# The second RMS norm's factor is taken out of the turned x and put back at the gate and behind the down product

## The reference, cut to what matters

```
x = x + m @ w_out                                      # 2048 x 2048
h = x * rsqrt(mean(x*x, axis=-1) + 1e-6) * norm2_w     # the second norm: one factor r per token
x = x + (silu(h @ w_ffn_gate) * (h @ w_ffn_up)) @ w_ffn_down   # 2048 x 5632, twice, and 5632 x 2048
```

## Time and profile before

| | |
|---|---|
| time, median of 3 runs | 2487.36 us (2487.17 to 2497.38) |
| time of the profiled execution | 2485.11 us |
| its span in the profile | 2483.2 us |
| PE busy | 2417.0 us, 97% of the span |
| DVE busy, ACT busy, POOL busy | 1518.9, 1130.0, 194.4 us |
| granted TensorE clock over the span | 0.994 of full speed |

### The profile page before, as it was taken

How to read it: one execution, slowest core, us unless ns; L and a number is a source line. 1 busy time by engine, 2 the same in 40 slices (tenths; PEclk the granted TensorE clock), 3 DMA queues, 4 the chain that set the end, 5 groups by cost and what they waited for, 6 DMA issues and landing times.

```text
span 2483.2 us, 42677 instructions
## 1 busy us (share of the span) xinstructions
PE 2417.0 (97%) x18297; PEld 2147.6 (86%) x18297; DVE 1518.9 (61%) x1890; ACT 1130.0 (46%) x1562; POOL 194.4 (8%) x198
## 2 busy tenths in 40 slices
PE   7999999999999999999999999999999999999997
PEld 7777889999888888888888899889888899899886
DVE  4899955565555655556544445745745568456556
ACT  5565545554444444444443434533544535334442
POOL 4000000001000000000000001220000061301000
PEclk9999999999999999999999999999999999999998
DMA  8444454455646666666666676434537674335465
GB/s 238 136 145 144 153 153 128 128 171 184 194 148 190 183 184 197 188 193 188 193 189 192 189 224 179 120 99 118 168 103 238 176 215 140 98 109 151 126 198 170
DMA packets 259405, 412.28 MB, mean 166 GB/s; under 512 B 53072, under 2 KB 74064, under 8 KB 258704
## 3 DMA queue, kind: packets, MB, share of 16 engines
q1 hardware_dynamic: 254496, 395.57, 53.6%
q0 software_dynamic: 4400, 13.89, 2.0%
q10 hardware_dynamic: 320, 0.08, 0.0%
HBM read 403.17 MB, written 6.30 MB: 165 GB/s over the span
## 4 chain that ended last, share of the span: by engine, by line
PE 89%; DVE 6%; ACT 2%; issue 2%; DMA 0%; ACTq 0%; SPq 0%; DVEq 0%
PE banks L578 88%; DVE wp_hl L1126 2%; ACT wp_hl L1808 1%; DVE r_SA L1664 0%; PE banks L801 0%; DMA xt<-x 0%; DVE r_SA L1630 0%; DVE rsd L1275 0%; DVE nsd L1542 0%; DVE r_kb L1632 0%; ACT L1808 0%; PE banks L695 0%; DVE xr L1801 0%; DVE xr L1799 0%; DVE sqr L1285 0%
## 5 line engine op out<-in xcount | busy, mean ns | idle before, releaser
L578 PE MATMUL banks<-XX_hl,wp_hl 128*128 128x256 f32 (+1 forms) x10112 | 1424.7, 300 | 10.4 <-DVE wp_hl L1126 9.2
L1126 DVE TENSOR_TENSOR wp_hl<-raw,wp_hl 128x1024 fp32r<-128x1024 f32 x740 | 913.9, 1242 | 826.3 <-ACT wp_hl L1808 825.7
L578 PEld LDWEIGHTS banks<-XX_hl,wp_hl 128*128 128x128 f32 x10112 | 1319.7, 190 | 89.7 <-issue 15.4
L1808 ACT ACTIVATE wp_hl<-raw 128x1024 fp32r<-128x1024 f32 x740 | 781.4, 1059 | 1057.3 <-PE banks L578 1034.5
L578 PE MATMUL banks<-wp_hl,FF_hl 128*128 128x512 f32 x1056 | 240.4, 389 | 0.0
L578 PEld LDWEIGHTS banks<-wp_hl,FF_hl 128*128 128x128 f32 x1056 | 197.9, 188 | 41.0
L578 PE MATMUL banks<-wp_hl,XX_hl 128*128 128x512 f32 x576 | 139.1, 398 | 0.0
L578 PEld LDWEIGHTS banks<-wp_hl,XX_hl 128*128 128x128 f32 x576 | 107.6, 190 | 28.1 <-issue 5.3
L578 PE MATMUL banks<-wp_hl,MXa_hl 128*128 128x512 f32 x384 | 88.3, 389 | 0.0
L578 PE MATMUL banks<-wp_hl,MM_hl 128*128 128x512 f32 x384 | 87.4, 389 | 0.0
L578 PEld LDWEIGHTS banks<-wp_hl,MM_hl 128*128 128x128 f32 x384 | 71.9, 188 | 15.2 <-DVE wp_hl L1126 0.3
(11 more groups left out here) (432 smaller groups left out, 1884.3 us busy)
## 6 DMA issues: line engine op xcount, KB each, us to landing
raw<-w_in SPq DMA_DIRECT2D x304, 512.0 KB, 3.8
raw<-w_out SPq DMA_DIRECT2D x96, 512.0 KB, 4.5
raw<-w_ffn_gate SPq DMA_DIRECT2D x88, 512.0 KB, 4.3
raw<-w_ffn_up SPq DMA_DIRECT2D x88, 512.0 KB, 4.2
raw<-w_ffn_down SPq DMA_DIRECT2D x88, 512.0 KB, 4.2
raw<-w_proj_attn SPq DMA_DIRECT2D x16, 512.0 KB, 4.2
raw<-w_proj_ssm SPq DMA_DIRECT2D x16, 512.0 KB, 3.7
raw<-w_glu SPq DMA_DIRECT2D x8, 512.0 KB, 3.7
```

Of the source, the lines that this page charges most:

```text
L578: return e.matmul(o, lhsT, rhs, start=start, stop=stop, skip_group_check=True)
L1126: return tt(d, src, hi, SUB)
L1808: return e.activation(o, x, func, bias=bias, scale=scale)
```

## The change

The turned x is no longer scaled: each quarter of `wo` is turned three pieces later with the identity, in the middle of the next job, and the factor comes in at two other places. As a row over all partitions, `rrow` (ones times the diagonal, a product on PE and a copy), it is multiplied into the summed gate, before the Silu; as a scalar per partition it is multiplied into the down product where that is added to x. The up product stays unscaled, since the factor at the end makes up for it. `wo3` isn't treated apart any more, and ACT's early load of the table for the square root is gone.

```diff
-    HALF, HLF = ("wo3", "xo30", "xo31"), marks("half", "h")
+    HALF, HLF = ("xo30", "xo31"), marks("half", "h")
...
+    RRT, RRV, FGV = marks("rrow_t", "t"), marks("rrow_v", "c"), marks("f_norm", "r")
...
     # PE, turned_x
-            if stage < 2:
+            if stage == 0:
                 e.wait_ge(*XD("d", stage))
-            elif stage == 2:
-                e.wait_ge(*freed(f"fd{g // 2}", 1))
+            elif stage < 3:
+                e.wait_ge(*freed(f"{('wo', 'fd')[stage - 1]}{g // 2}", 1))
...
-                    if stage < 2:
+                    if stage == 0:
                         last = mm(B[b][:, o:o + 128], src, dg[:, 128 * t:128 * t + 128], o == 0, o == 384)
                     else:
                         last = e.transpose(B[b][:, o:o + 128], src, ident)
...
     # PE, its list
         at.limit("wo3")
-        main(at.until("wo3"))
-        at.limit("fd3")
-        entered(1)
+        for c in range(4):
+            main(at.until(f"wo{c}"))
+            if c == 3:
+                at.limit("fd3")
+            main(at.go(6))
+            turned_x(1, 2 * c)
+            turned_x(1, 2 * c + 1)
+        bank(4, *RRV("c"))
+        e.wait_ge(*XD("d", 1))
+        for t in range(2):
+            last = mm(B[4][:, 128 * t:128 * t + 128], M["ones"], dg[:, 128 * t:128 * t + 128], t == 0, t == 1)
+        last.then_inc(RRT.made("t"), 1)
...
     # DVE, evac of wo and fd
-                    tt(x, x, b[i], ADD).then_inc(s_evV, 1)
+                    if n == "wo":
+                        tt(x, x, b[i], ADD).then_inc(s_evV, 1)
+                    else:
+                        stt(out=x, in0=b[i], scalar=rs[:, 2 + i:3 + i], in1=x, op0=MUL, op1=ADD).then_inc(s_evV, 1)
...
     # DVE, evac of fg, behind its four reductions
+                for i in range(2):
+                    g = v2(gt[2 * (c % 2) + i])
+                    e.wait_ge(*RRV("c"))
+                    e.wait_ge(s_evV, j.freed[2 * i + 1][1])
+                    tt(g, g, wide3(rrow, 2, 256), MUL).then_inc(FGV.made("r", 2 * c + i), 1)
...
     # DVE, its list
-        main(at.until("wo3"))
-        at.limit("fd3")
-        split(OF["wo3"].over + 2)
-        roots(1)
-        for g in range(10):
-            if g < 8:
-                rest_of_x(1, g)
-            if g > 1:
-                main(at.go(2))
+        for c in range(4):
+            main(at.until(f"wo{c}"))
+            if c == 3:
+                at.limit("fd3")
+            main(at.go(6))
+            if c == 3:
+                roots(1)
+            rest_of_x(1, 2 * c)
+            rest_of_x(1, 2 * c + 1)
+        e.wait_ge(*RRT("t"))
+        e.tensor_copy(rrow, B[4][:, 0:256]).then_inc(RRV.made("c"), 1)
...
     # ACT, evac of fg
-                    e.wait_ge(s_evV, j.freed[2 * i + 1][1])
+                    e.wait_ge(*FGV("r", 2 * c + i))
                     act(gt[2 * (c % 2) + i], gt[2 * (c % 2) + i], ACT.Silu).then_inc(FGA.made("s", 2 * c + i), 1)
...
     # ACT, its list
-        main(at.until("wo2"))
-        e.preload_act_table(ACT.Sqrt)
-        main(at.until("wo3"))
-        at.limit("fd3")
-        roots(1)
-        for g in range(10):
-            if g < 8:
-                rounded_x(1, g)
-            if g > 1:
-                main(at.go(2))
+        for c in range(4):
+            main(at.until(f"wo{c}"))
+            if c == 3:
+                at.limit("fd3")
+            main(at.go(6))
+            if c == 3:
+                roots(1)
+            rounded_x(1, 2 * c)
+            rounded_x(1, 2 * c + 1)
```

More of the change, by code:

```diff
@@ L313, in program @@
     FF = Pair("FF", 44 * T)
-    gt = [alloc(f"gt{i}", 512) for i in range(4)]
+    gt, rrow = [alloc(f"gt{i}", 512) for i in range(4)], alloc("rrow", 256)
     at[0] = (ARENA - 1024) // 8 * 8
@@ L1264, in main @@
                 if i:
-                    if p + 3 < NP and not (t + 1 == ENDS[j.name] and j.name in ("wo3", "xo30")):
+                    if p + 3 < NP and not (t + 1 == ENDS[j.name] and j.name == "xo30"):
                         split(p + 3)
```

## The result

| | before | changed |
|---|---|---|
| median | 2492.67 us (8 runs, 2484.73 to 2497.38) | 2502.18 us (8 runs, 2500.41 to 2504.45) |
| profiled execution, span | 2485.11, 2483.2 us | 2503.97, 2502.2 us |
| granted clock over the span | 0.994 | 0.991 |

The ratio is 1.0044, with a 95% interval of 1.0032 to 1.0056: 0.44% slower, within the half percent. It goes with the means, which differ by 11.0 us; the medians differ by 9.5, or 0.38%. The eight times of before are three from ahead of the prediction and five taken beside the changed kernel; their median is 5.3 us above that of the first three.

A forecast was written before the change was run, and what follows sets the result against it. PE, busy 97% of the span, was taken to bound the kernel. Gate 9.7 and front 1.0 make 10.7 us more, from a median of 2487.4 to 2498 us (0.43% slower); range 2490 to 2504.

The forecast's parts named there:

- its likeliest case: Whole kernel: front and gate terms hold, median 2495 to 2502 us; the forecast of 2493 to 2499.8 had chance 0.48.
- The first wait of the front: Between wo3 and fg0: PE stands still until the additions free wo3's banks, starting 3.65 us behind the last matmul.
- The second wait: In fg0, behind the last two turns: PE idles 2.88 us for the diagonal, the root's table load hidden.
- The clock: At the front's two waits: first fall costs about 2.75 us again, second 0 to 2.75, taken as 1.4.
- the full 2.75 worse: At the front: by the skill's rule of paying each long wait anew, two waits instead of one cost 2.75 us more.
- A wait under 1.8 leaves the clock alone: At PE's gate waits: waits of about 0.85 us, below 1.8, do not bring the granted clock down.
- The front as a whole: From wo3 into fg0: 0.4 us gained, 1.4 lost to the clock, +1.0 us in sum, ends -3.2 and +3.6.
- Its rival, that early turning gives the wait back: At the front: PE runs from wo3 into fg0 without a stop, median 2491.7 us; chance 0.07.
- The gate: Behind gate jobs: Silus 1.19 us later, PE stands still 0.85 behind ten jobs and 1.19 behind fg2: 9.7 us.
- the 2 and the 13 that the prediction names as signs of being wrong: PE's idle time from 740 to 1215 us: near 2 us refutes the gate part, above 13 the slack of 0.34.
- The down product: On DVE at the down job's addition: scalar with two inputs takes 676 ns against 0.68 us plain, so costs nothing.
- the unit: PE's time for one piece of a wide job, read from ACT's splits as 2.77 us each.

The follow-up runs named there:

- e2: The changed kernel without the products at the gate, the Silus waiting for the reductions as before: 2491.55 us, ratio 0.9998 to before.
- e5: The changed kernel with wo3 treated apart again and the factor made behind the first piece of fg0, two pieces earlier: 2494.85 us, ratio 1.0021 to before.
- e1: The kernel before plus only the two gate products per gate job, by a row of ones, the Silus waiting for them: 2503.62 us, ratio 1.0036 to before.
- e3: The changed kernel with the two Silus of a gate job put behind ACT's next split, all products kept: 2493.05 us, ratio 0.9998 to before.
- e8: The kernel before, unchanged, run once more for a second profile: 2492.35 us in one run, gate stretch 475.0 us.
- e6: The changed kernel with the edits of e3 and e5 together: 2480.55 us, ratio 0.9968 to before.
- e7: As e6, with the small operations of the angles spread over three pieces as well: 2476.97 us, ratio 0.9962 to before.
- e9: As e7, with four of the turns put between wo3 and fg0 to cover PE's wait there: 2484.42 us, ratio 0.9972 to before.
- e10: As e9, with the ones product ahead of the last two turns instead of behind them: 2476.11 us, ratio 0.9937 to before.
- e4: The kernel before with the angles' small operations spread over three pieces and ACT's sine and cosine four pieces later: 2486.84 us, ratio 0.9974 to before.

## Why the prediction was right, and where its steps were not

The forecast was 0.43% slower with 2498 us; measured are 0.44% and 2502.18. That lies in the stated range of 2490 to 2504, but above the 2493 to 2499.8 of the forecast and 0.2 above the 2495 to 2502 of its likeliest case. By its steps:

- **The first wait of the front** was to be 3.65 behind the last matmul of `wo3` and ended by the additions. It was 3.97 and ended by them. The additions were done 3.62 behind that matmul, where the sum has 3.59, but PE went on 0.35 behind them where the sum has 0.06. The gate waits do not show this delay.
- **The second wait**, 2.88 forecast, is 2.80, and the table load lies where the sum has it, hidden. By the drain that the Trainium skill adds to a load (ScalarE: Activation LUTs, "What ACT_TABLE_LOAD costs") the root would have come 1.2 us later, an estimate; the trace has it 0.06 behind the end of the load.
- **The clock** fell twice, which I had left half open. That costs 3.1 us and not the 4.15 of my sum (2.75 and 1.4), because less work ran at half clock in each fall (3.2 and 3.0 us) than in the one of before (5.75). The rule that each long wait pays anew (the Trainium skill, TensorE: Matmul & The Clock Gate, "HAM oscillation — how this bites in real kernels") holds here for waits of 3.97 and 2.80. What the prediction made of it, the full 2.75 worse, doesn't: it is some 0.35 worse. "A wait under 1.8 leaves the clock alone" held in the gate stretch, where waits up to 2.02 left it at 1.00, but not everywhere, as the last section shows.
- **The front as a whole**: +1.0 forecast, +0.08 in the profiles, and e2's 0.9998 says the same. The miss is that of the clock's term. Its rival, that early turning gives the wait back, failed on the banks of `wo3`, as argued; e5 shows what was to be had with another order, 8.6 us.
- **The gate**: 1.19 later on ACT is 1.20 in the trace. The lateness of PE behind `fg0` is 0.88 by the sums of DVE (23.34 for `fu0`, less 22.19 and five pieces at 0.053 more), against 0.85. Where PE had come at the slower pace the wait is 0.16 shorter, since it wants the fourth piece later. Four waits of 0.88, six of 0.72 and 1.19 behind `fg2` are 9.0 us; forecast were 9.7. The idle time shown, 7.9 us, lies between the 2 and the 13 that the prediction names as signs of being wrong. e1 and e3 show the cause from both sides.
- **The down product** was to cost nothing: from the sums of `fu10` to the addition of `fd3` are 242.09 us before and 242.08 in the changed kernel.
- **What the prediction did not know** is the second pace. Of the 14.47 us of the gate stretch 9.0 are waits; the other 5.4 are about 101 pieces at 0.053 more. The step that failed is the unit, PE's time for one piece of a wide job, 2.77 us, taken as a constant. The same hid in the base: the first profile of before was of its lower group, and the one of e8, of the usual upper group, has the slower pace for the 131 pieces behind the wait after `fg2`, 7.0 us. The two nearly cancel in the ratio: against the 475.0 of e8 the changed kernel loses 7.5 in the gate stretch and e1 8.7. Three of the eight times of before are of the lower group; an estimate with that mix is 10.1 lost at the gate, near the 11.0 by which the means differ. So it is in part luck that the ratio came out at the forecast 0.43%. The absolute time is 4 us above for the same reason, as far as the profile shows: 2498 with 5.4 for the pace, less 0.7 at the gate and 0.9 at the front, is 2501.8.

The rest of the difference of the two profiles, 2.0 us ahead of `wo0` and 2.4 behind `fd3`, lies in code that is the same in both. Ahead of `wo0` the changed kernel's profile shows the clock falling (a mean of 0.66) where before's does not (1.00); first before, then changed:

```profile
360.00:370.00 10.00, 9.88 (x52) 7.15 (x52) 4.79 (x15) 6.01 (x12) 0.00 (x0) 1.00 0.20 55
```

```profile
360.00:370.00 10.00, 10.00 (x41) 7.79 (x41) 4.23 (x12) 5.02 (x11) 0.00 (x0) 0.66 0.13 46
```

Single profiles differ by some microseconds in this way, which is why the times of many executions, not the spans, carry the verdict.

## What to carry to other kernels

Removing what a wait is named after is not removing the wait: ask which chain ends next, and on what the next job's first step still waits. Where two engines work in order for a third, added work on the one costs what it delays in the other's list; the Silus moved behind one split took away ten waits at no cost. And before a few microseconds are explained, compare the interval of the steady state in more than one profile; here the same program runs at two paces.

## What was not expected of the hardware

- PE runs the same stream of wide fp32 matmuls (a job has 64 of 512 and 64 of 256 columns) at 2.77 or at 2.83 us per piece, at a granted clock of 1.00, and keeps the one it has until the stream is broken. Behind a wait of 0.5 to 2 us either can come: behind `fg2` in before the slower one came in 49 of 70 executions, by their times. Behind a break without a wait the matmuls in it and the pace ahead of it seem to decide: with the ones product last the pace changed over in four of four profiles (e5, e6, e7, e9), and all 12 times of e9 lay at 2482 to 2487; with the identity turns last it stayed the faster one in e10, with 6 of 6 times at 2475 to 2477; and the turns by the diagonal, last in before, e1 and e4, were followed by the faster one in all four profiles. What makes the difference inside PE stays open.
- A wait of 2.80 us brought the clock down, at the end of the wait. One of 1.73 that ended at 359 us in the changed kernel was followed, behind 2.6 us of small matmuls, by a fall; in before the same wait (it ended at 360) was followed by none. So the length of one wait alone does not tell whether the clock falls.
- PE went on 0.35 us behind the end of DVE's addition that freed a bank, and 0.36 in e5, where the clock was 1.00 all the while; behind a low part of a weight piece it went on after 0.05. Why isn't known.
